# Opening of a two-block transformer kernel: the last modulation rows summed on VectorE, the query tile fetched between their halves, the small vectors issued first

## What is computed

```python
shift, scale, gate = jnp.split(jax.nn.silu(c) @ w_mod + b_mod, 3, axis=-1)
shift_c, scale_c, gate_c = jnp.split(jax.nn.silu(c_ctx) @ w_mod + b_mod, 3, axis=-1)
hx = rmsnorm(x, g_pre) * (1 + scale[:, None]) + shift[:, None]
hc = rmsnorm(ctx, g_pre) * (1 + scale_c) + shift_c
q, k, v, ga, uf, gf, zc, bc, cc, gc = split_cols(hx @ w_in, PROJ_SIZES)
...
```

## Time and profile before

| what | us |
|---|---|
| median of three runs | 1997.35 |
| lowest, highest run | 1996.68, 2002.61 |
| the profiled execution, its own time | 2000.51 |
| its span in the profile | 1998.6 |
| PE busy in it | 1937.0 (97%) |
| DVE, ACT, POOL busy | 799.0, 827.2, 702.1 |
| first product of the first query tile starts at | 50.33 |
| first product of the second query tile starts at | 68.66 |

### The profile page before, as it was taken

How to read it: one execution, slowest core, us unless ns; L and a number is a source line. 1 busy time by engine, 2 the same in 40 slices (tenths; PEclk the granted TensorE clock), 3 DMA queues, 4 the chain that set the end, 5 groups by cost and what they waited for, 6 DMA issues and landing times.

```text
span 1998.6 us, 26892 instructions
## 1 busy us (share of the span) xinstructions
PE 1937.0 (97%) x10454; PEld 1637.8 (82%) x10454; DVE 799.0 (40%) x1830; ACT 827.2 (41%) x1571; POOL 702.1 (35%) x552
## 2 busy tenths in 40 slices
PE   8999999989999999999999999999999999999997
PEld 4898889877788888877888888888887898888885
DVE  3555556442546435476511111017367551111004
ACT  3221268355238446577233222125477533223211
POOL 1523312125452135310544454445321245444452
PEclk9999999999999999999999999999999999999999
DMA  9544311112331124310333333322420223333321
GB/s 278 172 161 145 136 43 44 28 47 85 106 128 42 34 65 129 89 54 22 85 100 90 106 86 126 106 77 91 122 80 23 63 65 106 106 86 104 127 84 43
DMA packets 198117, 183.72 MB, mean 92 GB/s; under 512 B 31686, under 2 KB 166204, under 8 KB 197992
## 3 DMA queue, kind: packets, MB, share of 16 engines
q1 hardware_dynamic: 191960, 170.67, 27.7%
q10 hardware_dynamic: 6032, 11.33, 1.8%
HBM read 179.86 MB, written 5.40 MB: 93 GB/s over the span
## 4 chain that ended last, share of the span: by engine, by line
PE 84%; DVE 7%; ACT 3%; issue 2%; POOL 2%; DMA 1%; SPq 0%; ACTq 0%; DVEq 0%
PE ps L1302 23%; PE ps L1304 23%; PE ps L1303 23%; PE ps L1391 3%; PE ps L1809 2%; PE ps L1886 2%; POOL w_lo L722 2%; PE ps L1358 1%; PE ps L1377 1%; PE ps L1904 1%; PE ps L1421 1%; DVE sc L2465 1%; ACT w_hi L776 1%; PE ps L1336 1%; DVE qc L2496 1%
## 5 line engine op out<-in xcount | busy, mean ns | idle before, releaser
L722 POOL TENSOR_TENSOR w_lo<-raw,w_hi 128x512 fp32r<-128x512 f32 (+1 forms) x518 | 680.3, 1344 | 1193.0 <-ACT w_hi L776 1192.9
L776 ACT ACTIVATE w_hi<-raw 128x1024 fp32r<-128x1024 f32 (+2 forms) x261 | 258.7, 1037 | 265.2 <-PE ps L1304 203.8
L1302 PE MATMUL ps<-g_hi,w_lo 128*128 128x512 f32 (+1 forms) x928 | 348.4, 375 | 1.5 <-POOL w_lo L722 1.5
L1303 PE MATMUL ps<-g_lo,w_hi 128*128 128x512 f32 (+1 forms) x928 | 347.5, 374 | 0.0
L1304 PE MATMUL ps<-g_hi,w_hi 128*128 128x512 f32 (+1 forms) x928 | 347.5, 374 | 0.0
L1302 PEld LDWEIGHTS ps<-g_hi,w_lo 128*128 128x128 f32 x928 | 174.7, 188 | 33.8 <-issue 1.7
L1304 PEld LDWEIGHTS ps<-g_hi,w_hi 128*128 128x128 f32 x928 | 174.7, 188 | 31.3
L1303 PEld LDWEIGHTS ps<-g_lo,w_hi 128*128 128x128 f32 x928 | 174.7, 188 | 30.9
L1302 PE MATMUL ps<-h_hi,w_lo 128*128 128x512 f32 (+1 forms) x496 | 180.3, 364 | 4.0 <-DVE h_lo L2027 2.3
L2591 DVE TENSOR_TENSOR tmp_f<-ps,tmp_f 128x512 f32<-128x512 f32 x44 | 30.4, 692 | 370.7 <-PE ps L1304 370.7
L1304 PE MATMUL ps<-h_hi,w_hi 128*128 128x512 f32 (+1 forms) x496 | 174.6, 352 | 0.0
(11 more groups left out here) (283 smaller groups left out, 3466.4 us busy)
## 6 DMA issues: line engine op xcount, KB each, us to landing
raw<-in_w_in SPq DMA_DIRECT2D x30, 1024.0 KB, 5.1
raw<-in_w_mod SPq DMA_DIRECT2D x24, 1024.0 KB, 6.9
raw<-in_w_gate SPq DMA_DIRECT2D x44, 512.0 KB, 4.0
raw<-in_w_up SPq DMA_DIRECT2D x44, 512.0 KB, 5.2
raw<-in_w_down SPq DMA_DIRECT2D x22, 1024.0 KB, 4.9
raw<-in_w_out SPq DMA_DIRECT2D x8, 1024.0 KB, 5.0
strips<-bias_rows ACTq DMA_DIRECT2D x18, 256.0 KB, 3.7
raw<-in_w_in SPq DMA_DIRECT2D x16, 256.0 KB, 4.4
```

The source lines that it names most:

```text
L722: pool.tensor_tensor(w_lo[:, i % SPLIT, a:e], raw_of(what)[:, a:e], w_hi[:, i % SPLIT, a:e].bitcast(F32), ALU.subtract).then_inc(s_tile_lo ...
L776: act.activation(w_hi[:, i % SPLIT, a:b], raw_of(what)[:, a:b], ACT.Copy).then_inc(s_tile_hi.sem, s_tile_hi.nth((what, n)))
L1302: pe.matmul(o, lhs[1], rhs[0], start=first, stop=False)
L1303: pe.matmul(o, lhs[0], rhs[1], start=False, stop=False)
```

## The change

Eight things are changed, all before the second query tile:

1. The last pair of modulation tiles (3 and 7) is no longer multiplied on PE. The same 2 MB come as two half tiles, each with 512 rows of both (`last_rows_tile`), and DVE weighs them (`weigh_last(0)`, `weigh_last(1)`, eight instructions each) into two new accumulators `acc_first`; PE sums those (`sum_last_rows`) and DVE adds the bias (`last_rows_in`).
2. The first query tile moves from place 8 of the stream to place 7, between the half tiles (places 6 and 8).
3. On PE two `first_mod` and two `first_turn` are gone; `q0_rows(0, 0)` now stands before the turning of blocks 4 and 5, `q0_rows(0, 1)` to `(0, 3)` before the sum, blocks 6 and 7 are turned after it, and four `q0_rows` are left for after that.
4. On ACT two row copies are gone, and the root of x's norm stands before the fourth row copy.
5. On DVE the norms of x stand before `first_in(3)`; `weigh_last(0)` stands after `first_rows(1)` and `weigh_last(1)` after `first_rows(2)`.
6. On POOL the first two pieces of the query tile's low part stand after the second `ctx_lo` instead of the fourth, the third and fourth piece one pair later each.
7. SP waits for `weigh_last(0)` before the second query tile, for the query tile's low part before the constants, and for `weigh_last(1)` before the tile after the next.
8. On SP the small vectors stand before the first tile and before the second, not after them.

```diff
-        FIRST = [(0, "mod", j) for j in (0, 4, 1, 5, 2, 6, 3, 7)]
+        FIRST = [(0, "mod", j) for j in (0, 4, 1, 5, 2, 6)]
+        LAST_ROWS = [(0, "last rows", kh) for kh in range(2)]
+        def last_rows_tile(kh):
+            return (LAST_ROWS[kh], [(lambda r, i=i: r.rearrange("p (k c) -> p k c", k=4)[:, :, 256 * i:256 * i + 256],
+                                     I["w_mod"][0][512 * kh:512 * kh + 512, 256 * j:256 * j + 256].rearrange("(k p) c -> p k c", p=P))
+                                    for i, j in enumerate((3, 7))], False)
...
-                mix = first + mix
+                mix = first + [last_rows_tile(0), mix[0], last_rows_tile(1)] + mix[1:]
...
-                    elif stream[n - RAW][0] in WEIGHED:
+                    elif stream[n - RAW][0] in WEIGHED + LAST_ROWS:
...
-                for into, src in loads:
-                    sp.dma_start(into(raw[:, n % RAW, :]), src).then_inc(landed_sems[n % RAW], 16)
                 if n < 2:
                     for dst, src in vectors[4 + 5 * n:9 + 5 * n]:
                         sp.dma_start(dst, src).then_inc(s_vectors.sem, 16)
+                for into, src in loads:
+                    sp.dma_start(into(raw[:, n % RAW, :]), src).then_inc(landed_sems[n % RAW], 16)
...
-                if m > 0:
-                    tile_lo_part(0, 2 * m - 2)
-                    tile_lo_part(0, 2 * m - 1)
+                if m == 0:
+                    tile_lo_part(0, 0)
+                    tile_lo_part(0, 1)
+                else:
+                    tile_lo_part(0, m + 1)
...
             squares(0, 2)
+            root((0, "pre", "x"), 8, XT)
             first_row(3)
-            root((0, "pre", "x"), 8, XT)
...
+            def sum_last_rows():
+                pe.wait_ge(*emptied[LAST_BANK])
+                emptied[LAST_BANK] = s_mod_in.after((0, KD // 2 - 1))
+                pe.wait_ge(s_weigh.sem, s_weigh.at(LAST_ROWS[1]))
+                for h in range(2):
+                    for c in range(4):
+                        o = 256 + 2 * c + h
+                        m = pe.matmul(ps[:, LAST_BANK, o:o + 1], acc_first[h][:, P * c:P * c + P], ones[:, 0:1], start=True, stop=True)
+                m.then_inc(s_mod.sem, s_mod.nth("last rows"))
...
-            first_mod(6)
+            q0_rows(0, 0)
             turn_x(0, 4)
             turn_x(0, 5)
             turn_ctx(0, 1)
-            first_turn(6)
-            first_mod(7)
+            q0_rows(0, 1)
             turn_ctx(0, 2)
-            first_turn(7)
-            q0_rows(0, 0)
+            q0_rows(0, 2)
+            q0_rows(0, 3)
+            sum_last_rows()
             turn_x(0, 6)
             turn_x(0, 7)
-            q0_rows(0, 1)
+            q0_rows(0, 4)
             turn_ctx(0, 3)
-            for k in range(2, KD):
+            for k in range(5, KD):
                 q0_rows(0, k)
...
+            def weigh_last(kh):
+                what = LAST_ROWS[kh]
+                if kh == 0:
+                    dve.wait_ge(s_cond.sem, s_cond.at(0))
+                wait_landed(dve, what)
+                for k in range(4):
+                    for h in range(2):
+                        to, w = acc_first[h], raw_of(what)[:, 512 * k:512 * k + 512]
+                        by = cond[:, 4 * kh + k, h:h + 1]
+                        if kh == 0 and k == 0:
+                            V.tensor_scalar(to[:], w, by, None, ALU.mult).then_inc(s_weigh.sem, s_weigh.nth((what, k, h)))
+                        else:
+                            dve.wait_ge(s_weigh.sem, s_weigh.at((what, k - 1, h) if k else (LAST_ROWS[0], 3, h)))
+                            V.scalar_tensor_tensor(to[:], w, by, to[:], ALU.mult, ALU.add).then_inc(s_weigh.sem, s_weigh.nth((what, k, h)))
+                s_weigh.name_latest(what)
...
-            first_in(3)
             inverse((0, "pre", "x"), 8, XT)
             for t in range(XT):
                 first_norm(t)
+            first_in(3)
...
             first_rows(1)
+            weigh_last(0)
             first_shift(2)
-            first_in(6)
             first_rows(2)
-            first_in(7)
+            weigh_last(1)
+            last_rows_in()
             first_shift(3)
             first_rows(3)
```

26 lines of the change are left out of this document (17 added, 9 removed).

## The result

| | kernel before | changed kernel |
|---|---|---|
| median of six runs each, us | 2002.39 | 2009.12 |
| lowest, highest run | 1996.68, 2003.65 | 2007.21, 2010.57 |
| profiled execution, its own time; span | 2000.51; 1998.6 | 2008.85; 2007.0 |
| first product of the first query tile | 50.33 | 42.01 |
| first product of the second query tile | 68.66 | 74.99 |

The ratio of the two kernels' times, from all these runs, is 1.0044, with a 95% interval of 1.0030 to 1.0057 (the quotient of the two medians alone is 1.0034). By the medians the changed kernel is slower by 6.7 us, and its 2009.1 stands against a forecast of 2000.0 and at most 2006.5.

A forecast was written before the change was run, and what follows sets the result against it. PE, busy 1937.0 of 1998.6 us, was taken as the bound. The second query tile at +0.8 or +3.5 us, with 0.5 for the clock, gave a middle of +2.6 and forecast 2000.0; 8-in-10 range 1995.0 to 2006.5.

The forecast's parts named there:

- The path that decides: DVE's work up to PE's sum: `h_lo`, two weighings, scale and shift; second weighing done at 57.9 or 60.6 us.
- the taking of turns: DVE and POOL alternate during the second weighing, adding two ctx low parts and a query piece; it ends at 60.6 us.
- the prediction's two ends: End of the second weighing on DVE: 57.9 us if DVE keeps POOL out, 60.6 if they alternate.
- POOL comes too late: Rival, chance 0.21: POOL's first query piece waits for the whole first weighing; second query tile +7 us, time 2005.5.
- No crowding: Rival, chance 0.12: DVE loses nothing to POOL and the clock holds; second query tile at 66.4 us, time 1994.5.
- the price of 0: Later constants, later tiles and DVE's later weighing after the opening cost 0, at most 3 us without DVE's spare time.
- The clock: PE falling to 1.2 GHz in the opening's first idle time, costing up to 5 us, hidden but for about 0.5.
- the fall in the second idle time: Rival, chance 0.09: sum and four channel blocks run at 1.2 GHz for up to 10 us, losing up to 5; 2005.
- The first fall comes first and fills it: Argument against half clock at the sum: the slow stretch starts in PE's earlier gap, with 10 us at 0.50 expected.
- It is hidden: First four channel blocks, up to 5 us slower, end at about 58 where DVE delivers; only about 0.5 us shows.
- The earlier root and the vectors: Opening: norms some 2 us sooner, small vectors delay the tile stream by 0.8; tile 5's product starts 1.1 us earlier.
- The yardstick: Base for the forecast time: 1997.35 us, median of three runs; the profiled execution took 2000.51.

The follow-up runs named there:

- POOL held: Changed kernel with POOL waiting for the second weighing before ctx's low parts of blocks 4 and 5 and the last query piece; 2005.8 us, ratio 1.0016.
- first idle time filled: Changed kernel with 18 small products on PE behind the turning of the sixth modulation tile's rows, before the first query product; 2006.1 us, ratio 1.0022.
- second idle time filled: Changed kernel with 20 small products on PE ahead of its wait for the second weighing, before the sum; 2003.9 us, ratio 1.0009.
- weighing cut: Changed kernel with only one of four pieces of each half tile weighed, so its modulation rows are wrong; 1999.7 us, ratio 0.9988.
- all remedies: Changed kernel with weighing split around `h_lo`, POOL waiting for the second weighing, turning ahead of the sum, 18 products before the first query product; 2001.8 us, ratio 0.9996.
- turning before the sum: Changed kernel with the turning of x's blocks 6 and 7 and ctx's last pair and the fifth channel block ahead of the sum; 2004.8 us, ratio 1.0014.

## Why the prediction was wrong

**The path that decides: right, its end partly by luck.** The sum's wait, 5 to 7 us, was foreseen and measured 5.83; weighing ended at 60.14, where the taking of turns gave 60.6; the first query product started at 42.01 (42.6), the query tile landed at 39.5 (40). Instructions that meet POOL grew to 1.76 us from 0.74. With POOL held the second weighing is 1.96 us shorter, where the prediction's two ends were 2.7 apart. The luck is in the parts: the sixth modulation tile came at 31.36, not at 32.5, and DVE began the first weighing at 40.36, not at 41.6; the first half-clock stretch, which had no term on DVE's path, took this back, and the second weighing began at 52.80 (52.5). Two sums of the prediction are off by 0.2 and less, to no effect: 48.6 + 1.5 + 0.6 + 1.3 + 1.3 is 53.3 and not 53.1, and 1997.35 + 7 + 1 is 2005.35 and not 2005.5.

"POOL comes too late" did not happen: POOL's first pieces came at 40.70, 0.34 us behind the start of the first weighing, and took 2.68, though the rival had them wait for the whole weighing in just this order. "No crowding" is refuted by the same rows. Behind the opening the price of 0 held.

**The clock: the step that failed.** It stood in the sum with 0.5, with the fall in the second idle time as a rival at 0.09, which is what happened, at 3.15 us and not "up to 5". Both parts of its reasoning fell:

- "The first fall comes first and fills it": it lasted 6.8 us, not the 10 read from one row, and ended at 46.5, eight microseconds before the second idle time began. With the first idle time filled, the second fall still came. Measured price 3.15.
- "It is hidden": the first channel block at half clock held up the turning of ctx, by that ACT, and by that the second weighing. Measured price 1.3 to 1.9, from one execution. PE's own idle time was taken as the only cover, and who waits for the slowed products was not asked.

With 1.33 for the first, the two cost 4.5 us together instead of 0.5. The remainder of the +6.33, 74.99 - 68.66 - 3.15 - 1.33 = 1.85, lies inside the +0.8 to +3.5 that was worked out for everything but the clock.

The Trainium skill, "TensorE: Matmul & The Clock Gate", section "Why this matters for your kernels", wants no gaps over some 3 us between bursts of matmuls. The 5.05 and 5.83 us here agree with it; a shorter idle time, the 2.38 us ahead of the sum with the turning first, had its fall too. The prediction named the rule and argued it away with a mechanism that no row showed: the earlier trace rows show one idle time and one stretch, and no second idle time behind it.

**The earlier root and the vectors: right in direction, not in their parts.** Together they were put at 1.1 us for the sixth modulation tile, 1.9 for the root less 0.8 for the vectors. In the kernel before they give 1.6 together (33.59 to 31.97), 1.3 for the root alone and 0.3 for the vectors alone, which cost nothing; for the second query tile the root alone gives 1.4. This gain is contained in the 1.85, so putting two modulation tiles on DVE costs about 1.85 + 1.71 = 3.6 us even with the clock's part taken off (1.71 = 68.66 - 66.95, from the kernel before with vectors and root early), or 3.0 if the first fall cost 1.9. That is worked out by difference and was not measured alone.

**The yardstick: the larger part of the miss.** Of the 9.1 us between 2000.0 and 2009.1, 5.0 are the median of three, 1997.35, against 2002.4 with more runs; 4.1 are the change, 6.7 instead of 2.65, for which the clock's 4.5 instead of 0.5 accounts. Added to 2002.4 the same working would have given 2005.0. The profile's own execution, 2000.51, had been the hint that 1997.35 was low.

## What to carry to other kernels

A stage of matmuls that is made to start earlier but then waits twice for another engine pays more than the waits: here two idle times of 5 and 6 us cost another 4.5 us in products at 1.2 GHz behind them. Before placing work behind a gap, see who waits for the first products after it; and treat each gap as having its own fall. Undoing a chain that holds up a copy by order alone (a root that stood too late on ACT) was worth more, 1.4 us in the opening, than moving 2 MB of multiplications to an engine with time to spare.

## What was unexpected in the hardware

- **Gaps of 1.5 to 2.9 us were followed by a fall, and not every time.** After a gap of 1.50 to 1.73 us at 24 to 26 us the clock was at 0.50 from 27 on in four profiles (second idle time filled, POOL held, weighing cut, all remedies), and stayed at 1.00 in two (the changed kernel, turning before the sum), with the same instructions up to there. PE's timeline of the first of these:

```profile
25.66 0.60 PE L1439 MATMUL ps<-fold,mod_row 2*128 2x2 f32 x4 [1.50 <-ACT mod_row L850]
26.19 5.30 PE L1431 MATMUL ps<-raw,cond 128*2 128x256 f32 x16
```

  The changed kernel has the same gap, 1.49, and then 3.61 a product. Gaps of 0.46 to 0.55 at this place were not followed by a fall; but of the eight profiles that have them, seven also have a stretch at 7.3 to 8.9 (the eighth has no record of the clock before 10.6), so the length of the gap was not tested by itself. The idle time of 2.86 us at 436 us was followed by a fall in the second profile of the kernel before and not in the first. The sum's gaps: 5.83, 6.31, 3.88 and 2.38 us were followed by slow products, 0.86 us was not, and 2.39 (all remedies) was not at first: the clock fell 3 us after it, at 61.1.
- **A short half-clock stretch puts back all that follows.** The product of a modulation tile costs 5.30 us instead of 3.61 where the stretch at 27 covers its start, and in the four profiles that have it the first query product comes 1.2 to 2.2 us later than in the changed kernel.
- **DVE and POOL took turns instruction by instruction.** The Trainium skill, "SBUF — State Buffer", section "SBUF: two separate sides", has the shared ports locked for one whole instruction; the opening of the changed kernel agrees (weighing instructions of up to 1.76 us beside POOL, 0.74 alone), while the earlier trace rows of another place, POOL shut out for five instructions, do not. In the opening POOL was already at work when the weighing instructions that read two inputs began (40.70 before 42.17, and 52.28 before 52.80), and in the earlier trace rows it came while they ran. Whether that decides it was not tested.
